# A first block whose attention is spread over its last projection tiles, with pooling on TensorE and the row tiles cut in halves

## What is computed

```python
def first_block(x, p, ...):                 # 2 layers
    for i in range(DEPTH):
        z = rmsnorm(h, norm_g[i]) @ w_in[i] + b_in[i]
        (c_val, c_glu, c_gate, p_in, p_gate, q, k, v, a_gate, qi, ki, wi) = split(z)
        ya = conv_module(c_val, c_glu, ...) * silu(c_gate)      # 31 taps, layernorm, silu, 256x256
        yb = pool_mixer(p_in, ...) * silu(p_gate)               # running means over 2, 4, 8, 16
        yc = sparse_attention(rope(q), rope(k), v, rope(qi), rope(ki), wi) * silu(a_gate)
        h = h + concatenate([ya, yb, yc]) @ w_out[i]
        h = h + (p[i] @ ple_w[i]) * sigmoid(h @ ple_gate_w[i])
    return rmsnorm(h, final_norm_g)
```

## Time and profile before

| | us |
|---|---|
| median of 3 runs | 1675.71 |
| lowest, highest | 1674.61, 1675.8 |
| profiled execution, its own time | 1676.77 |
| its span | 1674.8 |

### The profile page before, as it was taken

How to read it: one execution, slowest core, us unless ns; L and a number is a source line. 1 busy time by engine, 2 the same in 40 slices (tenths; PEclk the granted TensorE clock), 3 DMA queues, 4 the chain that set the end, 5 groups by cost and what they waited for, 6 DMA issues and landing times.

```text
span 1674.8 us, 22758 instructions
## 1 busy us (share of the span) xinstructions
PE 1483.4 (89%) x9053; PEld 1243.3 (74%) x9053; DVE 960.2 (57%) x1801; ACT 717.5 (43%) x1170; POOL 71.4 (4%) x88
## 2 busy tenths in 40 slices
PE   5988887987887999977989999999979797799996
PEld 3975775974765878656668888888758784699996
DVE  4788645897555228454366556632262365588854
ACT  3434543445543256054244434422142635466642
POOL 0030000020000001100000000000000011000000
PEclk8997998997988999988989999999989899999998
DMA  5443646435544222411333332323232233455552
GB/s 208 164 137 128 216 162 230 163 116 190 192 138 171 92 76 97 152 43 64 110 105 100 101 101 91 95 91 102 74 130 95 80 102 121 152 168 184 178 185 91
DMA packets 61976, 217.50 MB, mean 130 GB/s; under 512 B 6864, under 2 KB 8912, under 8 KB 61872
## 3 DMA queue, kind: packets, MB, share of 16 engines
q1 hardware_dynamic: 59440, 206.60, 36.6%
q0 software_dynamic: 2288, 9.08, 1.7%
q10 hardware_dynamic: 144, 0.38, 0.1%
HBM read 214.98 MB, written 1.05 MB: 129 GB/s over the span
## 4 chain that ended last, share of the span: by engine, by line
PE 74%; DVE 12%; ACT 5%; DMA 4%; issue 3%; SPq 0%; DVEq 0%; ACTq 0%
PE bank L509 19%; PE bank L511 19%; PE bank L510 19%; DMA RAWB<-in_ws 4%; PE bank L480 2%; DVE WLO L1498 2%; PE bank L530 2%; PE bank L531 2%; PE bank L532 2%; DVE CV L1671 1%; DVE NLO L1791 1%; PE bank L597 1%; DVE L L1574 1%; DVE TB L1783 1%; PE bank L894 1%
## 5 line engine op out<-in xcount | busy, mean ns | idle before, releaser
L509 PE MATMUL bank<-NHI,WHI 128*128 128x256 f32 (+1 forms) x1808 | 596.9, 330 | 56.8 <-DVE WLO L1498 18.7
L510 PE MATMUL bank<-NLO,WHI 128*128 128x256 f32 (+1 forms) x1808 | 587.1, 325 | 0.0
L511 PE MATMUL bank<-NHI,WLO 128*128 128x256 f32 (+1 forms) x1808 | 586.5, 324 | 0.0
L1498 DVE TENSOR_TENSOR WLO<-RAWB,WHI 128x1024 fp32r<-128x1024 f32 (+1 forms) x302 | 362.9, 1206 | 331.4 <-ACT WHI L1059 329.2
L509 PEld LDWEIGHTS bank<-NHI,WHI 128*128 128x128 f32 x1808 | 352.7, 195 | 95.7 <-issue 54.1
L1059 ACT ACTIVATE WHI<-RAWB 128x1024 fp32r<-128x1024 f32 (+1 forms) x302 | 310.2, 1031 | 261.2 <-PE bank L511 171.2
L510 PEld LDWEIGHTS bank<-NLO,WHI 128*128 128x128 f32 x1808 | 353.6, 196 | 25.9 <-issue 1.9
L511 PEld LDWEIGHTS bank<-NHI,WLO 128*128 128x128 f32 x1808 | 353.1, 195 | 24.9
L1059 ACT ACTIVATE CF<-bank,PRM 128x512 f32<-128x512 f32 (+1 forms) x88 | 59.1, 672 | 184.9 <-PE bank L511 184.9
L2097 DVE SCALAR_TENSOR_TENSOR CF<-bank,PRM,CF 128x510 f32<-128x510 f32 (+1 forms) x88 | 54.1, 615 | 113.6 <-ACT CF L1059 112.3
L509 PE MATMUL bank<-HHI,WHI 128*128 128x512 f32 (+1 forms) x352 | 119.1, 338 | 0.0
(11 more groups left out here) (253 smaller groups left out, 1664.2 us busy)
## 6 DMA issues: line engine op xcount, KB each, us to landing
RAWB<-in_ws SPq DMA_DIRECT2D x366, 512.0 KB, 3.5
RAWB<-in_ws SPq DMA_DIRECT2D x32, 384.0 KB, 3.1
NB<-in_nab POOLq DMA_DIRECT2D x12, 256.0 KB, 3.7
K<-in_c POOLq DMA_DIRECT2D x2, 896.0 KB, 4.8
X<-in_xt SPq DMA_DIRECT2D x4, 256.0 KB, 4.9
X<-in_xt POOLq DMA_DIRECT2D x1, 1024.0 KB, 6.3
out_x<-X SPq DMA_DIRECT2D x1, 1024.0 KB, 4.8
K<-in_c POOLq DMA_DIRECT2D x1, 832.0 KB, 11.9
```

What stands on the lines that cost most here:

```text
L509: nc.tensor.matmul(o, hi[:, w], xh, start=(i == 0), stop=False)
L510: nc.tensor.matmul(o, hi[:, w], xl, start=False, stop=False)
L511: ins = nc.tensor.matmul(o, lo[:, w], xh, start=False, stop=(i == slabs - 1))
L1498: V.tensor_tensor(WLO[:, k % SPL, 0:w], RAWB[:, u % RAW, 0:w], WHI[:, k % SPL, 0:w].bitcast(F32), ALU.subtract).then_inc(S("lo_ready"), 1)
```

## The change

- **Tiles.** ki and wi become one tile `kiwi` (25 tiles in place of 26), and the order is val, glu, kiwi, qi, qa, ka, qb, kb, pin, agate, cgate, pgate (qa: the first half of q). `NATIVE_FROM = NZ1`, so every tile is still split in hi and lo.
- **Attention.** The steps of `attend(k)`, k = 0 to 10, follow the tiles 14 to 24 on each of the three engines. An item goes through scores, transposes and product with V in three successive steps. Scores have two banks in place of four. ACT does the normalisation, after DVE's reciprocal. Taps and the end of the top-64 search stand in the same steps.
- **Pooling.** In place of POOL's chain: transposes (`pool_turn`), products with a matrix of windows (`pool_means`) and the mixing matrix (`pool_mix`) on PE behind tiles 17, 18 and 20, all in bank 5, with copies on ACT (`UT`, `PD`, `YP`) behind tiles 18, 19 and 21.
- **Tail of the layer.** The first `ple` unit runs ahead of `w_out`; the first two tiles of `w_out` run side by side, slab by slab (`fm_side_by_side`), the convolution's slabs last; hi and lo of the new x are made tile by tile; the second `ple` unit follows `w_out`. V's bias moves to the attention's output, V's copy to ACT.
- **Row tiles.** In the first block: four halves behind tiles 2, 5, 9 and 12 (two row tiles a layer), one at the start of layer 1, one at the end. One in place of two at the start of the second block and before the up projection of its layer 0. Nine, in 18 halves, in that up projection (tiles 4, 6, ..., 38).
- **Up projection** in both layers: its first two tiles side by side.

```diff
+TILES1 = ["val"] * 2 + ["glu"] * 2 + ["kiwi"] + ["qi"] * 2 + ["qa"] * 2 + ["ka"] * 2 + ["qb"] * 2 + ["kb"] * 2 + \
+    ["pin"] * 2 + ["agate"] * 4 + ["cgate"] * 2 + ["pgate"] * 2
+NATIVE_FROM = NZ1
+ATTEND_FROM = 14
+ROTATE_AT = {5: 0, 7: 1, 9: 2, 11: 3, 13: 4, 15: 5}
+ROWS1 = (2, 5, 9, 12)
+TAPS_AT = {5: (0, 2), 7: (2, 3), 9: (3, 4)}
+TAPS_BESIDE = {2: (4, 5), 3: (5, 6), 4: (6, 7), 5: (10, 11), 6: (14, 15), 7: (18, 19), 8: (22, 23), 9: (26, 27)}
+TAPS_AFTER = {4: (7, 10), 5: (11, 14), 6: (15, 18), 7: (19, 22), 8: (23, 26), 9: (27, CONV_K)}
+ITEMS1 = [(pr, qt, P * (qt + 1)) for qt in range(TT) for pr in range(NH1 // 2)]
+UP_ROWS = 9
+def up_half(l, m):
+    return l == 0 and m % 2 == 0 and 4 <= m < 4 + 4 * UP_ROWS
...
+                for t in range(NZ1):                       # PE
+                    ...fm...
+                    if t in ROWS1:
+                        i = ROWS1.index(t) % 2
+                        rows(5, 4 * i, 4 * i + 4)
+                    if t in (7, 14):
+                        columns(5)
...
+                    if t in ROTATE_AT:
+                        rotate(ROTATE_AT[t])
...
+                    if t >= ATTEND_FROM:
+                        attend(t - ATTEND_FROM)
+                    if t == 17:
+                        pool_turn()
+                    if t == 18:
+                        pool_means()
+                    if t == 20:
+                        pool_mix()
+                channel_mean(4, CV, "conv_ready", "xc_ready")
+                pe.wait_ge(S("ple_split"), l + 1)
+                ple()
+                channel_mean(5, CT, "conv_sq", "cvar_eps")
+                fm_side_by_side(2, T, x_lat, "wo_freed", "y_split", Y_ORDER, 6, conv_mix)
+                for m in range(2, KS):
+                    fm(KS, T, x_lat, "wo_freed")
+                ple()
...
+                fm_side_by_side(AHEAD, n, rhs, "up_freed", "x_split")
+                columns(5)
+                for m in range(AHEAD, 2 * FT):
+                    fm(KS, n, rhs, "up_freed")
+                    if up_half(l, m):
+                        rows(5, 2 * (m % 4), 2 * (m % 4) + 4)
+                    if m % 4 == 3 and up_half(l, m - 1):
+                        columns(5)
...
                 for p in range(FT + 2):                    # ACT
                     if p < FT:
                         for w in range(2):
-                            unit()
+                            unit(1, 2 if up_half(l, 2 * p + w) else 0)
...
                             A(CF[:, w, p % 3, 0:n], bank[me.next_tile()][:, 0:n], ACT.Identity,
                               bias=prm_col(f"fb{l}", j), scale=prm_col(f"fw{l}", 2 * FT + j)).then_inc(S("centre_ready"), 1)
+                        if p % 2 == 1 and up_half(l, 2 * p):
+                            copy_rows(5, me.u - 1)
...
+                def attend(k):                             # ACT
+                    if 1 <= k <= n:
+                        ...
+                        act.wait_ge(S("pt_ready"), me.nth("pt_ready"))
+                        A(PT1[...], bank[4]...).then_inc(S("pt_freed"), 1)
+                    if k < n:
+                        act.wait_ge(S("l_ready"), me.nth("l_ready"))
+                        ...Exp..., then_inc(S("e_ready"), 1)
+                        act.wait_ge(S("r_ready"), me.nth("r_ready"))
+                        ...Identity, scale=ST1[:, s, 3, e:e + 1])....then_inc(S("p_ready"), 1)
...
+                    if t >= ATTEND_FROM:                   # ACT, tile loop
+                        attend(t - ATTEND_FROM)
+                    if t == 13:
+                        act.wait_ge(S("rl_used"), me.nth("rl_used", 2))
+                    if t == 18:
+                        act.wait_ge(S("ut_turned"), l + 1)
+                        A(UT[:].rearrange("p t c -> p (t c)"), bank[5][:]).then_inc(S("ut_ready"), 1)
...
+                def attend(k):                             # DVE
+                    if k < n:
+                        ...tensor_tensor_reduce x2, l_ready...
+                        if k in TAPS_BESIDE:
+                            taps(*TAPS_BESIDE[k])
+                        if k == 1:
+                            rope(5, "qk_roped")
+                        dve.wait_ge(S("e_ready"), me.nth("e_ready", 2))
+                        V.reciprocal(ST1[:, s, 3, :], ST1[:, s, 2, :]).then_inc(S("r_ready"), 1)
+                    ...
+                    if k < 4:
+                        topk(1, 2 * k, 2 * k + 2)
+                    if k in TAPS_AFTER:
+                        taps(*TAPS_AFTER[k])
...
+                    if t in (8, 15):                       # DVE, tile loop
                         modulation(5)
...
+                    if t in (10, 12, 14):
+                        ...rope(t // 2 - 3, "qk_roped")
+                    if t == 12:
+                        topk(0, 0, 3)
+                    if t == 13:
+                        topk(0, 3, 6)
+                    if t == 14:
+                        topk(0, 6, 8)
```

More of the change, by code:

```diff
@@ new lines, in pool_means @@
+                def pool_means():
+                    pe.wait_ge(*held[5])
+                    for m in range(2):
+                        for t in range(TT):
+                            for e in range(2):
+                                g = 2 * m + e
+                                win = c1v("win0")[:, g * T:(g + 1) * T] if t == 0 else c1v("win1")[:, g * P:(g + 1) * P]
+                                ins = nc.tensor.matmul(bank[5][half(e), m * T + t * P:(m + 1) * T],
+                                                       UT[:, t, m * P + 64 * e:m * P + 64 * e + 64], win, start=(t == 0), stop=(t == 1))
+                    ins.then_inc(S("pd_made"), 1)
+                    read_by(5, "pd_ready")
@@ L715, in _ @@
-                attention(ITEMS1, score1, L1, lambda e: (4, e * T), pv1, between=beside)
-                rows(4)
-                pe.wait_ge(S("pool_ready"), me.nth("pool_ready"))
-                for m in range(2):
-                    if 2 + m in held:
-                        pe.wait_ge(*held[2 + m])
-                    ins = nc.tensor.matmul(bank[2 + m][:, 0:T], M1[:, 512 + m * P:512 + (m + 1) * P], PD[:, m, :],
-                                           start=True, stop=True)
-                    ins.then_inc(S("pw_ready"), 1)
-                    read_by(2 + m, "pw_freed")
@@ new lines, in out, with silu @@
+                def out(i):
+                    for pr in (2 * i, 2 * i + 1):
+                        ins = A(OB[:, pr, :], bank[6 + i][:, pr % 2 * T:(pr % 2 + 1) * T], ACT.Identity, bias=prm_col(f"bv{l}", pr))
+                    ins.then_inc(S("o_freed"), 1)
+                def silu(name, g0, n):
+                    z = Z1[name]
+                    act.wait_ge(S("z_freed"), zb + z + n)
+                    for k in range(0, n, 2):
+                        ins = A(GT1[:, g0 + k:g0 + k + 2, :], Z[:, z + k:z + k + 2, :], ACT.Silu)
+                    ins.then_inc(S("silu_ready"), 1)
@@ new lines, in _ @@
+                    if t == 21:
+                        act.wait_ge(S("pw_ready"), me.nth("pw_ready"))
+                        act.wait_ge(S("pb_ready"), l + 1)
+                        for m in range(2):
+                            ins = A(YP[:, m, :], bank[5][:, m * T:(m + 1) * T], ACT.Identity, bias=PB[:, m:m + 1],
+                                    scale=prm_col(f"pools{l}", m))
+                        ins.then_inc(S("yp_ready"), 1)
+                    if t == 22:
+                        act.wait_ge(S("pv_done"), 8 * l + 6)
+                        out(0)
+                        silu("agate", 4, 4)
@@ L1740, in _ @@
[L1740 to L1744 removed]
+                    gated(CT, (m,), 0, 0)
+                lows(CT, range(2), 0)
+                me.tile += 4
                 for m in range(KS):
```

712 lines of the change are left out of this document (384 added, 328 removed).

## The result

| | before | after |
|---|---|---|
| median of 5 runs, us | 1675.71 | 1683.29 |
| lowest, highest | 1674.61, 1680.29 | 1681.17, 1686.21 |
| span of the profiled execution | 1674.8 | 1681.1 |

The changed kernel is slower by 0.4%: the ratio is 1.0042, with a 95% interval of 1.0026 to 1.0059, so the difference is small but clear of the noise. I had forecast 1650.5 with a range of 1634 to 1668, so the time is outside it and on the other side.

A forecast was written before the change was run, and what follows sets the result against it. PE was taken to bound the kernel. Layer 0 (-23.0) and layer 1 (-24.5) of the first block, start (+0.5) and second block (+21.7) summed to -25.3 us: forecast 1650.5 us, range 1634 to 1668.

The forecast's parts named there:

- term (7): Up projection of layer 0, second block: nine row tiles cost halves 17.3, columns 7.3 and waits 13.5, +38.2 us.
- term (1): First block, first tile to first gate tile: new tile and attention order takes 162 us a layer, 19.4 and 13.6 less.
- rival A: Up projection: nine waits make the clock fall, 3.1 us each, +27.9, with some +6 in the first block: 1684; chance 0.10.
- three named places: First block, PE idle behind tile 15 (about 9 us), behind tile 18 (about 5) and ahead of channel_mean (about 5).
- rival B: First block: overlap gains little, the stretch stays at 172 instead of 162 us, +20, 1670; chance 0.15.
- The first of its reasons: First block, rival B: PE runs at half clock after each of the three places where it waits.
- the second holds in part: First block, rival B's other reason: the unit stream behind row halves lands late at 2.88 us a tile.
- My own sign for B: First block: over 168 us from first tile to first gate tile would show rival B (chance 0.15).
- Gate tiles: First block's gate tiles: columns behind the first tile and half clock at the start go, -2.8 and -3.9 us.
- front of layer 1: First block, gate to layer 1's first tile: V copied by ACT -0.8, one row tile landing sooner -6.2 us.
- up projection's front: Second block, layer 0: one row tile less ahead -6.4 us, first two tiles side by side -3.4.
- The second block's front: Start of the second block: one row tile instead of two lets TB start sooner, -6.2 us.

The follow-up runs named there:

- e1: Changed kernel with PE running a row tile's columns one tile later in the up projection, in a bank of their own: 1656.61 us, ratio 0.9877.
- e8: Changed kernel with the nine row tiles of the up projection left out: 1633.23 us in one run.
- e3: Changed kernel with ACT copying the turned pooling input and the means ahead of its attention steps at tiles 18 and 19: 1668.84 us, ratio 0.9944.
- e12: Changed kernel with edits of e1 and e3, rotation in bank 4, reordered rope and taps, two plain fp32 tiles, two row tiles moved to the first block: 1632.36 us.
- e7: Changed kernel with ACT copying the up projection's row tile behind the silu, which lengthens PE's waits: 1683.81 us in one run.

## Why the prediction was wrong

**Two steps failed, term (7) and term (1).** The first took 13.3 us more than counted, the second 16.4 in its two layers. Either alone would have left the time inside my range (1664 and 1667 us); both together gave the other sign.

**Term (7), the row tiles in the up projection.** I counted 38.2 us and it was 51.5. The mechanism was right and in its place: nine waits released by ACT's ROWS, 1.36 us each plus the 0.16 of overlap. Two sizes were off. The work itself is 3.3 us a row tile and not 2.73 (e1 against e8), which makes 4.8 us. And the clock: four tiles 1.6 us longer, 6.4. The last 2 us go with the wait as well (22.1 against 12.2 of gaps, 1.4 of overlap and 6.4 of slow tiles); the columns behind a wait, 1.05 us instead of 0.95, are 0.9 of them. I had put that clock loss into rival A at 3.1 us for each of nine and given it 0.10, because one gap of 1.34 us in the earlier trace rows was followed by full speed. One gap was too little: in the changed kernel five of nine gaps of that size are followed by full speed as well. The right sum would have been a share of nine, and A was an "all or nothing" case where the truth lay between. That A's time, 1684, is the measured one is luck: its 27.9 us of clock in the up projection were 6.4, the clock there was 0.98 and not below 0.95, and the rest of the miss lies in the first block.

Beside that one gap I had the Trainium skill (TensorE: Matmul & The Clock Gate, section "A second HAM failure mode: psum-queue depth-cycling"), which reports of a bf16 kernel that its clock oscillates because PE idles briefly and often between groups of matmuls. The traces agree in part: it happened behind four of nine gaps of 1.36 us, none of nine of 0.69, one of nine of 1.87.

**Term (1), the stretches: 169.8 and 170.5 where I laid out 162.** All three named places came as named (9.06, 5.42, 4.90 us; forecast about 9, 5, 5). Up to the channel mean, layer 0, PE's trace counted from start to start has 107.8 us of work where I had 99.7, and 20.6 us of idle time where the layout had 22.8. Of the 8 us the tiles are 6.0 (78.0 for 72; 2.0 of it at reduced clock, 4.0 at full clock, about half of that in the first matmul behind other work) and the rotations 2.9. The pooling, for which I had no row, took 3.9 us of PE for 4.6. In detail:
- A rope's rotation of 512 columns was set at 0.46 us; it takes 1.10 us of PE (the next matmul starts 1.03 later), the short one 0.60 instead of 0.25. A row half takes 1.06 and not 0.96. Tile 12 starts 44.9 us behind the first tile instead of 42; three rotations, the short one and three halves ahead of it are 2.4 of the 2.9.
- DVE's gaps behind the first two places are 2.97 and 4.71 us, not 1.8 and 3.9.
- The channel mean so came at 128.4 instead of 122.5. From there to the gate it was 41.5 instead of 39.5. The ple unit took 5.07 us, mostly at half clock, where I had 2.85, but hidden, and in e3 it takes 4.1 at a tail of 39.7; the 2 us are the half clock behind the fourth wait, which my layout didn't have.

I had given the cold clock 0.8 us a layer. e3, with the pooling wait gone, has 3.7 us less of busy PE in layer 0, 2.4 of it behind the channel mean, where the fourth wait is. So rival B (172, at 0.15) was the nearest of my cases for this part. The first of its reasons, half clock after each place, is in the trace; the second holds in part: behind the halves ACT waits up to 4.01 us for a unit, but outside the three waits PE idles for only 1.2 us up to the channel mean. My own sign for B, over 168 us in the stretch, came.

Small slips of the recorded sum: the parts of PE's 99.7 add to 99.4, those of (7) to 38.1; and the prices 0.68 and 1.14 are from one start to the next, where the rows show durations of 0.78 and 1.22. None of them matters here.

**Parts that held.** Gate tiles -2.6 and -3.7 (forecast -2.8, -3.9); front of layer 1 -7.1 (-7.0); up projection's front -10.0 (-9.8). The second block's front gave 3.9 of 6.2; the same code took 2.1 us less there in e1, e3, e8 and e12, so the rest is no error of the count.

**The sign.** The sum was two large terms against each other, about -63 and +38, and both were off the same way: 16 and 13 us. I had taken A and B as separate cases, either one enough to fill the range's upper end; they share one cause, PE stopping and restarting, and came together. Their common case had no place in my range or my chances. With A's own price of 3.1 us a gap it would have been 1698, with what (7) really missed, 13, and B's 20 it is 1683: the common case had to be there, but its size only the runs give.

## What to carry to other kernels

A copy that another engine needs must not be queued behind an instruction that itself waits: twice here copies of 0.6 us on ACT (two a layer in the first block, nine in the up projection) cost 14 and 22 us, and moving them, or their reader by one tile, gave that back. Where PE streams at full clock, price a wait as its length plus a chance of a slow restart, and take the restarts of all places as one rival, not as many. And before work is moved from idle gaps into a full stream, count it there at its measured period: nine row tiles cost 29.4 us in the stream with no wait at all, about what removing them elsewhere gave outside the tile stretches (2.6 + 7.1 + 3.7 + 3.9 + 10.0 = 27.3, some 3.4 of it from the up projection's first two tiles side by side).

## What was not expected of the hardware

- A longer gap can cost less clock than a shorter one: nine gaps of 1.87 us were followed by one slow tile (e7, one run), nine of 1.36 us by four in each of five kernels, and not behind the same waits. In the first block a gap of 2.83 us was followed by full clock (e3), one of 2.28 by half clock (after).
- Two kernels with the same matmuls in a stretch, in almost the same order, differ in PE's busy time by the clock (0.92 and 0.96): 144.82 us after, 141.09 in e3.
